# One inference step of a hybrid decoder on one core: the first gate weights earlier, two up blocks around the maximum over pages, and the attention branch's weights held back

## The reference

```
[u | q | k | v | forget | gate] = RMSNorm(x) @ W_in
x += W_out( sig(g_pool) * (PoolMixer(u) @ w_up_pool) + sig(g_att) * (Attention(q,k,v,logf) @ w_up_att) )
x += HierMoE(RMSNorm(x))     # 32 experts, width 512, top 2 inside the top group
y = RMSNorm_final(x)
```

## Time and profile before

| what | value |
|---|---|
| median of 3 runs | 713.39 us (712.56 to 715.01) |
| the profiled execution | 715.12 us, with a span of 713.3 us |
| PE busy | 593.0 us (83%) |
| DVE busy | 214.7 us (30%) |
| ACT busy | 91.3 us (13%) |
| moved by DMA | 269.17 MB, mean 377 GB/s |
| granted clock of TensorE, mean | 0.912 |

### The profile page before, as it was taken

One profiled execution on the slowest core, in us unless ns is written; L12 is line 12 of the kernel. 1 busy time (PEld: TensorE's weight loads), 2 busy tenths in 40 slices (PEclk: granted clock), 3 DMA queues, 4 the chain that ended last, 5 costly groups with the idle time before them and its releaser, 6 DMA issues.

```text
span 713.3 us, 13726 instructions
## 1 busy us (share of the span) xinstructions
PE 593.0 (83%) x6123; PEld 379.8 (53%) x6123; DVE 214.7 (30%) x523; ACT 91.3 (13%) x247; POOL 52.2 (7%) x58
## 2 busy tenths in 40 slices
PE   8999699999899989999776687767778767877883
PEld 7788577775488855545433344433444334443441
DVE  4159998852141252222111111111111111111113
ACT  3411234330000250000000000000000000000012
POOL 5135611022000000000000000000000000000000
PEclk9999899999999999999998889898889887898997
DMA  9996999966999869999999999999999999999982
GB/s 297 310 360 176 372 355 337 349 262 283 404 416 411 362 229 401 421 426 426 425 423 419 426 428 424 424 423 425 426 425 424 423 424 427 423 424 422 423 362 79
DMA packets 42403, 269.17 MB, mean 377 GB/s; under 512 B 9844, under 2 KB 10672, under 8 KB 23903
## 3 DMA queue, kind: packets, MB, share of 16 engines
q1 hardware_dynamic: 35616, 229.51, 80.3%
q0 software_dynamic: 3072, 35.19, 12.2%
q10 hardware_dynamic: 3655, 3.57, 1.5%
HBM read 266.02 MB, written 2.46 MB: 376 GB/s over the span
## 4 chain that ended last, share of the span: by engine, by line
DMA 66%; PE 26%; DVE 4%; issue 2%; ACT 1%; SPq 0%; DVEq 0%; POOLq 0%; ACTq 0%
DMA ring<-w_up 49%; DMA x<-w_up 6%; PE bank L1598 6%; DMA ring<-w_in 5%; PE bank L1657 4%; PE bank L1643 3%; DMA ring<-cache_v,ridx 2%; PE bank L1385 2%; DVE ring L1051 2%; DMA front<-q_scratch 1%; PE bank L1575 1%; PE bank L1494 1%; DMA q_scratch<-x 1%; PE bank L1485 1%; PE bank L1369 1%
## 5 line engine op out<-in xcount | busy, mean ns | idle before, releaser
L1385 PE MATMUL bank<-ring,front 128*32 128x256 f32 x1856 | 160.5, 484 | 85.4 <-DMA ring<-w_up 73.3
L1385 PEld LDWEIGHTS bank<-ring,front 128*32 128x32 f32 x1856 | 85.3, 138 | 145.8 <-issue 122.7
L1247 DVE COPY front<-bank 128x256 f32<-128x256 f32 x32 | 13.6, 425 | 232.6 <-PE bank L1385 232.6
L1598 PE MATMUL bank<-hT,ring 128*128 128x264 f32 x256 | 61.4, 396 | 7.0 <-DMA ring<-w_in 6.5
L1598 PEld LDWEIGHTS bank<-hT,ring 128*128 128x128 f32 x256 | 48.7, 194 | 17.5 <-DMA ring<-w_in 7.4
L876 ACT ACTIVATE front<-bank 128x128 f32<-128x128 f32 x32 | 8.9, 277 | 371.1 <-PE bank L1393 371.1
L1401 PE MATMUL bank<-ring,front 128*32 128x256 f32 x928 | 55.4, 379 | 0.0
L1369 PE MATMUL bank<-front 128*32 128x256 f32 (+1 forms) x768 | 52.9, 389 | 0.3 <-DVE front L1147 0.3
L1503 PE MATMUL bank<-hT,ring 128*128 128x264 f32 x192 | 44.3, 388 | 0.0
L1401 PEld LDWEIGHTS bank<-ring,front 128*32 128x32 f32 x928 | 30.0, 110 | 20.7 <-issue 1.1
L1257 DVE COPY front<-bank 128x256 f32<-128x256 f32 x32 | 13.6, 425 | 88.0 <-PE bank L1401 88.0
(11 more groups left out here) (312 smaller groups left out, 556.3 us busy)
## 6 DMA issues: line engine op xcount, KB each, us to landing
ring<-w_gate SPq DMA_DIRECT2D x28, 2048.0 KB, 14.8
ring<-w_up SPq DMA_DIRECT2D x28, 2048.0 KB, 14.7
ring<-w_down SPq DMA_DIRECT2D x28, 2048.0 KB, 14.7
ring<-w_in SPq DMA_DIRECT2D x8, 2048.0 KB, 24.1
x<-w_gate SPq DMA_DIRECT2D x3, 2048.0 KB, 14.7
x<-w_up SPq DMA_DIRECT2D x3, 2048.0 KB, 14.8
x<-w_down SPq DMA_DIRECT2D x3, 2048.0 KB, 14.8
ring<-w_out SPq DMA_DIRECT2D x2, 2048.0 KB, 20.0
```

The costliest lines, as they stand in the source:

```text
L1247: v.tensor_copy(gu.rearrange("p (c n) -> p c n", c=2), bank[GATEUP][:, 0:QUART].rearrange("p (n c) -> p c n", c=2)).then_inc(s_gusb, 1)
L1385: last = m.matmul(bank[GATEUP][32 * g:32 * g + 32, 0:256], xgT[:, k % 2, k // 2], w[:, k, 256 * (g % 2):256 * (g % 2) + 256], start=k == 0 ...
L1598: last = m.matmul(out[:, 0:TOK], w[:, k, cols], hT[:, k, 0:TOK], start=k == 0, stop=k == DK - 1)
```

## The change

Three edits. The item g0 is sorted to just ahead of K2 in STREAM, so g0 gets the slot of w0, K2 that of K0, K3 that of w1, and g2, K7, up 0 and the values after them change slots too. In PLAN, gate 14 goes ahead of dmax with up 0, up 1 follows dmax, and the other up blocks follow with two fewer after dpv 4. SP waits, before it issues w_up_att, until the seventh sample's values (V6) have landed.

```diff
-        PLAN += [("m1", 0), ("gate", 13), ("dmax", 0), ("gate", 14), ("dshift", 0), ("gate", 15), ("dsums", 0)]
-        for b in range(NS):
-            PLAN += [("dpv", b)] + [("datt", 0)] * (b == 4) + [("up", b - (b >= 4))] * (b != 4)
-        PLAN += [("datt", 1), ("up", DK - 1)]
+        PLAN += [("m1", 0), ("gate", 13), ("gate", 14), ("up", 0), ("dmax", 0), ("up", 1), ("dshift", 0), ("gate", 15), ("dsums", 0)]
+        for b in range(4):
+            PLAN += [("dpv", b), ("up", b + 2)]
+        PLAN += [("dpv", 4), ("datt", 0), ("dpv", 5), ("dpv", 6), ("dpv", 7), ("up", DK - 2), ("datt", 1), ("up", DK - 1)]
...
-        STREAM = sorted(uses, key=lambda item: PLAN.index(uses[item][0]))
+        STREAM = sorted(uses, key=lambda item: PLAN.index(uses["K", 2][0]) - 0.5 if item == ("g", 0) else PLAN.index(uses[item][0]))
...
+                    if item == ("up", 1):
+                        sp.wait_ge(s_pages[where["V", NS - 2]], loaded["V", NS - 2])
```

## The result

The change makes the kernel slower. Its median is 717.02 us (714.05 to 718.71, 20 runs) and that of the kernel before, run beside it, 714.75 us (711.95 to 718.48, 20 runs). The ratio of the runs is 1.0047, with a 95% interval of 1.0035 to 1.0059: some 2.5 to 4.2 us more. (The two medians alone, over all runs, would give 1.0032.) All ratios here leave out slow executions, of which there was one, of the kernel with the hold alone: 941.12 us at a granted clock of 0.556. I had forecast 711.1 us, with a range of 707.5 to 715.5, and a chance of 0.15 for slower.

What follows compares the result with a forecast made beforehand. The front stage, set by PE, was taken to bound the kernel. At dpv 7, -2.9 (lead) + 3.9 (part two) - 3.3 (part three) made it 2.3 us earlier: 711.1 us against the median of 713.39, range 707.5 to 715.5.

Steps and rivals of the forecast that it cites:

- The bound: Front stage, set by PE: ending it earlier ends the kernel about as much earlier, up to some 6 us.
- g0: At gate 0: issued at about 59.6, landing at 70 to 74, so the wait goes; whole stall worth 7.6 us.
- K2 and the softmax: Before keys 8: DVE waits 2.3 us for K2, delaying the first softmax; PE waits at pT 0, lead 3.1 at gate 2.
- g1, the step that failed: At gate 4: g1 lands at 103 to 106, leaving PE a lead of 2.9 us after the gate.
- Rival C: At gate 4: g1 lands at 107 to 108 as before, lead 0 to 0.7, time 713.3 to 714; chance 0.22.
- Part two: Two up blocks between m1 and gate 15: worth 0 on PE alone, but V4 to V7 start 3.9 us later.
- Part three: At dpv 7: with w_up_att held, V7 lands 24.3 after gate 15, not 27.6, a gain of 3.3 us.
- D: At gate 4: g1 lands at 109 to 112, gate starts 1.5 to 4.5 later, time 715.5 to 718.5; chance 0.16.

Runs made afterwards that it cites:

- the last check above: New load order, steps of before, w_up_att held until V7, not V6, has landed, against the kernel before the change: ratio 1.0009.
- the run with K5 held: New load order, w_up_att held behind V6, steps of before, K5's gather held until g1 landed, against the kernel before: ratio 0.9945, median 709.28 us.

## Why the prediction was wrong

**The bound.** Right. What the front stage gains or loses at the merges is what the kernel gains or loses: in the windows of after, the DMA engines are busy 0.61 and 0.85 of the time between 250 and 260 and between 260 and 270. In the 13 profiled executions the merges begin between 192.00 and 200.78, and what follows them takes 515.6 to 518.3 us whatever they did, so a front stage that is earlier or later passes on, within that spread.

**g0.** Right. It was issued at 56.84, a little before my 59.6, and landed 13.4 us later, and the wait at gate 0 went.

**K2 and the softmax.** Right in place, off in size. DVE waited 2.80 us for K2 (forecast 2.3). I had called g0 nearly through; it landed 8 us after K2 was issued. But I looked for PE's wait at pT 0, and it came a step earlier, in nat 3. So gate 1, which I had counted as cover, stood behind the wait: 3.9 us of waits, 1.6 of the lower clock in gate 1, and a lead at gate 2 of 0.80 and not 3.1. Without the wait for g1 gate 4 would have started at 106.34, a lead of 1.4: this step alone took half of the 2.9 that I had counted on there.

**g1, the step that failed, together with nat 3.** "I take a landing of 103 to 106 and a lead of 2.9 us after gate 4": it landed at 107.4 and the lead was 0.3. I argued that 2 MB less ahead of it in its queue cancels 2 MB more in the gathers' queue. It did: from g1's issue to its landing the gathers moved 9.64 MB for 8.30 before, and the loads of SP 2.35 for 3.64. So g1 landed as before, and not earlier as I then took it: the gathers of K5 and K6 stand at its end in both kernels, and without them it lands 11 us sooner. Its landing alone caps the lead at 0.3, and nat 3 alone at 1.4; to move nat 3 and leave g1 where it was gained nothing. Rival C had g1's part, at 0.22, and not that of nat 3.

**Part two.** The price of 3.9 us was right in kind: 3.27 measured plus the lead of 0.29 is 3.56. My sum carried it, but with a lead of 2.9 set against it.

**Part three, mis-sized.** V7 after gate 15: forecast 24.3, measured 25.3. What is left isn't w_up_att, though it is issued at 186.65, with V7 still 5 us from landing: held until V7 was in (the last check above), it left V7 at 25.4 after gate 15 all the same. So the gathers' own term was too small. In that run they moved 8.39 MB between 163.6 and 188, a mean of 344 GB/s where I had put 426 and 3.6 us, and in the last 5 us the engines were busy 0.55 of the time. The gain is 2.3, not 3.3.

**Not in the sum.** The wait for V7 grew to 3.30 us, against the 2.5 I gave. I had asked about the clock behind the wait at pT 0, and not behind this one. It cost 0.88 on dpv 7 and 0.77 on up 6, 1.65 in all.

Put together: -0.29 + 3.56 - 2.33 is the 0.94 at dpv 7, and 1.65 more makes the 2.58 at the merges. I had -2.9 + 3.9 - 3.3 = -2.3. Of the difference of 4.9 us, the lead is 2.6 (nat 3 and g1 together), the clock 1.65, the hold 1.0, and the up blocks are -0.3. The runs' 2.5 to 4.2 us agree with the 2.58.

**The rival on the other side.** D, g1 later than before, wasn't what happened. The slower side came from a lead of nearly nothing, as in C, with a tail that cost 2.6 us at the merges, where I had let it cost 0.6 at most.

**The two transfers again.** K2 took 13.0 us where K3 had taken 13.8, and 11.0 in the run with K5 held; DVE waited 2.80 us and 0.80 for it. What sets K2's time isn't isolated, but it goes with g0's. In the seven profiled executions with the new load order in which g0 took 13.1 to 13.8 us, K2 took 12.9 to 13.6; in the other two g0 took 10.8 and 9.2, and K2 11.0 and 10.7. The Trainium skill (SBUF — State Buffer, SBUF: two separate sides) says that GpSimd can't write a gather's descriptors while DVE runs an operation that holds the port pair they share. No run here shows that the operations of keys hold it, and K2's time differed with the same keys beside it.

g1 goes from 35.4 to 24.4 us when two gathers are moved out of its way. The Trainium skill (DMA: Bandwidth & Descriptors, Queues, rings and completion order) says that the engines take turns between queues packet by packet. The trace agrees: beside K5 and K6 the two queues moved packets in like numbers (375 and 442) and very unlike amounts (4.33 and 0.87 MB).

## What to carry to other kernels

An order that fills a wait also delays every slot that is given back behind the filling: before work is moved ahead of a step, list the loads that wait for that step, and price them. A stall that is removed is worth only what the next waits leave; here the landing of g1 set the start of gate 4, at 106.7 to 108.8, in every kernel with the new load order that let the gathers of K5 and K6 go beside it, and the cure was to hold the two large gathers that shared its last ten microseconds. The best kernels here have the new load order, both holds and the old order of steps: 709.28 us, ratio 0.9945 to the kernel before (0.9942 with nat 3 moved as well, which is no difference), where the change has 1.0047.

## What the runs showed of the hardware

The time of a 2 MB load from issue to landing depends on what travels beside it. From w_in g0 took 9.2 to 13.8 us where it is issued ahead of the gathers of K2 to K6, and g1 took up to 36.9 us beside them. w_up_pool, of the same size, took 34.0 us beside the gathers of the values in one run and 12.6 in the kernel before, and w_up_att 8.2 us with no gather beside it.

Waits of nearly the same length cost differently. Behind the 1.94 us before dpv 7 the granted clock stayed at 1.00; behind 3.30 us it was 0.60 between 192 and 196, and the instructions after the wait took 1.65 us more. At gate 4 a wait of 3.00 us cost nothing in one run (the clock was 1.00 over the next 4 us, and gates 4 and 5 took 7.39 us as ever), and one of 2.91 us cost 1.7 in another (0.62, and 9.07 us). At gate 0 waits of 5.98 and 4.67 us made the gate 1.6 and 2.7 us longer. So in this kernel a wait of some 3 us can cost more than itself, and its length alone doesn't tell whether it will.
